# The prompt's own attention moved between the value tiles of the projection; eight equal steps a head in the attention stage

## The reference, cut to what matters

```python
# x_prompt: 128 tokens, x_sample: 1024 latent tokens, D = 1024, 8 heads; layer 1 is differential attention
qp, kp, vp, gp = attn_project(hp, w_in_attn)             # prompt: no rotary positions
op = diff_head_out(diff_attend(qp, kp, vp, lam), gp, subln, lam_init, w_out_attn)
qs, ks, vs, gs = attn_project(hs, w_in_attn)
qs, ks = apply_rope(qs), apply_rope(ks)
k_all, v_all = concat(ks, k_ctx), concat(vs, v_ctx)      # 1024 latent + 128 cached keys
os = diff_head_out(diff_attend(qs, k_all, v_all, lam), gs, subln, lam_init, w_out_attn)
# diff_attend: s = q k / sqrt(128) for both halves c of a head; p = softmax(s)
#              a = p[0] - lam * p[1];  o = a v
# diff_head_out: rms_norm(o) * subln * (1 - lam_init), then (o * silu(g)) @ w_out
```

## Time and profile before

| | us |
|---|---|
| median of 3 runs | 2426.21 (2423.43 to 2427.76) |
| the profiled execution | 2420.99 |
| its span | 2419.2 |
| TensorE busy | 2236.9 |
| VectorE busy | 1133.1 |
| ScalarE busy | 779.5 |

### The profile page before, as it was taken

How to read it: one execution, slowest core, us unless ns; L and a number is a source line. 1 busy time by engine, 2 the same in 40 slices (tenths; PEclk the granted TensorE clock), 3 DMA queues, 4 the chain that set the end, 5 groups by cost and what they waited for, 6 DMA issues and landing times. The chain is left out here.

```text
span 2419.2 us, 33660 instructions
## 1 busy us (share of the span) xinstructions
PE 2236.9 (92%) x13793; PEld 2138.6 (88%) x13793; DVE 1133.1 (47%) x1559; ACT 779.5 (32%) x1323; POOL 162.4 (7%) x68
## 2 busy tenths in 40 slices
PE   6799969988996999999999999989999999998996
PEld 1799947987996999999999999988888888888995
DVE  2835196374112644454411122237777777774112
ACT  2421043214112321111222121125666666664111
POOL 0200000000102121211200000000000000000100
PEclk9899889898998999999999999999999999999997
DMA  6554154177222445555542264361444443305224
GB/s 275 206 168 162 60 200 162 60 256 275 80 96 96 148 117 157 173 146 147 132 128 101 83 236 145 118 222 56 163 166 166 166 146 124 144 5 210 102 74 176
DMA packets 124603, 353.62 MB, mean 146 GB/s; under 512 B 12624, under 2 KB 62928, under 8 KB 116304
## 3 DMA queue, kind: packets, MB, share of 16 engines
q1 hardware_dynamic: 123344, 347.41, 41.8%
q10 hardware_dynamic: 1152, 4.72, 0.5%
HBM read 237.23 MB, written 114.82 MB: 146 GB/s over the span
## 5 line engine op out<-in xcount | busy, mean ns | idle before, releaser
L516 PE MATMUL p_ps<-p_h_hi,p_w_hi 128*128 128x384 f32 x1536 | 351.7, 336 | 33.3 <-DVE p_h_lo L616 33.3
L516 PE MATMUL p_ps<-p_h_lo,p_w_hi 128*128 128x384 f32 x1536 | 350.5, 336 | 0.0
L516 PE MATMUL p_ps<-p_h_hi,p_w_lo 128*128 128x384 f32 x1536 | 350.1, 335 | 0.0
L516 PEld LDWEIGHTS p_ps<-p_h_hi,p_w_hi 128*128 128x128 f32 x1536 | 275.4, 189 | 36.6 <-issue 28.5
L516 PEld LDWEIGHTS p_ps<-p_h_lo,p_w_hi 128*128 128x128 f32 x1536 | 275.5, 189 | 0.0
L516 PEld LDWEIGHTS p_ps<-p_h_hi,p_w_lo 128*128 128x128 f32 x1536 | 275.2, 189 | 0.0
L1371 PE MATMUL o_ps<-o_y_hi,o_w_hi 128*128 128x384 f32 x768 | 176.9, 338 | 25.3 <-DVE o_w_lo L1425 23.6
L1677 PE MATMUL a_ps<-a_v_hi,a_at_hi 128*128 128x256 f32 x584 | 178.8, 306 | 10.6 <-DVE a_g L1847 9.3
L1726 ACT ACTIVATE a_e<-a_ps,a_nmax 128x1152 f32<-128x1152 f32 (+1 forms) x143 | 161.3, 1128 | 69.6 <-DVE a_nmax L1792 69.6
L1792 DVE TENSOR_REDUCE a_nmax<-a_ps 128x1 f32<-128x1152 f32 (+1 forms) x143 | 176.3, 1233 | 4.0 <-PE a_ps L1640 1.6
L1371 PE MATMUL o_ps<-o_y_lo,o_w_hi 128*128 128x384 f32 x768 | 175.8, 336 | 0.0
(11 more groups left out here) (223 smaller groups left out, 3877.9 us busy)
## 6 DMA issues: line engine op xcount, KB each, us to landing
p_w_raw<-w_in_dram SPq DMA_DIRECT2D x40, 1024.0 KB, 6.1
g_dram<-p_stage SPq DMA_DIRECT2D x32, 576.0 KB, 3.0
f_w_raw<-w_u_dram SPq DMA_DIRECT2D x32, 512.0 KB, 3.6
o_w_raw<-w_out_dram SPq DMA_DIRECT2D x32, 512.0 KB, 4.3
f_g<-g_dram SPq DMA_DIRECT2D x8, 1152.0 KB, 7.7
y_dram<-f_y SPq DMA_DIRECT2D x8, 1152.0 KB, 5.3
x_dram<-o_x_new SPq DMA_DIRECT2D x16, 576.0 KB, 5.1
q_hi_dram<-p_cut_hi SPq DMA_DIRECT2D x32, 288.0 KB, 4.4
```

The source lines that it names most:

```text
L516: mm = pe.matmul(ps[:, 4 * b + c, 0:CH], a, x[:, c * CH:(c + 1) * CH], start=(d == 0 and j == 0), stop=(d == DT - 1 and j == 2))
```

## The change

The ninth step is taken out of the attention stage and done in the value unit of its head, and the rest follows from it:

- In a value unit the prompt's tile comes first (`ORDER`), then the eight latent ones. After the tile at place `at` TensorE, ScalarE and VectorE each do a piece of the prompt's attention of this head (`own_attention`): scores after place 0, maximum at 1, exponentials at 2, combination at 3, transpose and its two parts at 5, value product and norm at 6, scaling at 7, transposes of the output and gate at 8. Scores are now 128 columns wide. Two more PSUM banks (3 and 7) are used, and small tiles over parts of `stage` and of the past keys' split.
- SP loads the prompt's columns of q, k and g for head n + 1 at the start of unit n (`load_own`: four DMAs of 128 KB in 512-byte rows, one of 128 KB), and for head 0 in `after`, behind the first head's tiles. It first waits for the stores of all units ahead of the values. It stores the prompt's y of a head (`store_own`) one unit later.
- The value tiles are stored in the layout (head, partition, tile, column), in seven DMAs a unit (five and two) instead of six.
- In the attention stage every step has three groups and 1152 keys, 16 steps for two heads. `HeadTiles.load` takes 1024 queries, 1024 and 128 keys, twelve DMAs for a head; values have nine tiles, g and y the latent tokens only.
- 21 semaphores more are cleared between the two stages.

```diff
 class HeadTiles:
...
-            for what, size, into in (("q", T, self.q), ("k", KALL, self.k)):
+            for what, size, into in (("q", NS, self.q), ("k", KEYS, self.k)):
...
-            eng.dma_start(q, self.q_d[part][n, half]).then_inc(arrived, 16)
+            eng.dma_start(q, self.q_d[part][n, half][:, 0:NS]).then_inc(arrived, 16)
...
-            eng.dma_start(k[:, KEYS:KALL], self.k_d[part][n, half][:, NS:T]).then_inc(arrived, 16)
...
 def project(...):
...
+            SCORE, TURN = 3, 7
+            ORDER = [TT - 1] + list(range(TT - 1))
...
                 sp.wait_ge(past_out, 16 * 4)
+                for b in range(2):
+                    sp.wait_ge(stored[b], plan[3]["stored"][b])
                 ahead(sp)
+                load_own(0)
+
+            def load_own(n):
+                s = n % 2
+                for tiles, src in zip(own_qk, (heads.q_d, heads.k_d)):
+                    for tile, part in zip(tiles, src):
+                        sp.dma_start(tile[:, s].bitcast(F32), part[n].rearrange("c p t -> p c t")[:, :, NS:T]).then_inc(own_in[s], 16)
+                sp.dma_start(own_g[:, s], heads.g_d[n][:, :, NS:T]).then_inc(own_in[s], 16)
...
+                        if n >= 1:
+                            store_own(n - 1)
+                        if n + 1 < H:
+                            load_own(n + 1)
...
-                        for t in range(TT):
-
-                            pe.wait_ge(drained[p], k["drain"][p] + i * TT + max(t - 2, 0))
+                        for at, t in enumerate(ORDER):
+                            pe.wait_ge(drained[p], k["drain"][p] + i * TT + max(at - 2, 0))
...
                             mm.then_inc(proj_done, 1)
+                            own_attention(n, at, k["drain"][p] + i * TT)
...
+            def own_attention(n, at, drained_ahead):
+                s = n % 2
+                if at == 0:
+                    pe.wait_ge(own_in[s], 80 * (n // 2) + 80)
+                    pe.wait_ge(own_gated, n)
+                    for half in range(2):
+                        for j, (a, x) in enumerate(passes(*(part[:, s, half, :] for part in own_qk[0]),
+                                                          *(part[:, s, half, :] for part in own_qk[1]))):
+                            mm = pe.matmul(ps[:, SCORE, half * P:(half + 1) * P], a, x, start=(j == 0), stop=(j == 2),
+                                           skip_group_check=True)
+                    mm.then_inc(own_scored, 1)
+                if at == 5:
+                    pe.wait_ge(own_combined, n + 1)
+                    pe.wait_ge(own_scaled, n)
+                    pe.transpose(ps[:, TURN, 0:P], own_e[:, 0, :], sh.ident[:, :]).then_inc(own_turned, 1)
+                if at == 6:
+                    pe.wait_ge(own_lo, n + 1)
...
+                        mm = pe.matmul(ps[:, TURN, P:P + UC], a, x, start=(j == 0), stop=(j == 2), skip_group_check=True)
+                    mm.then_inc(own_multiplied, 1)
+                if at == 8:
+                    pe.wait_ge(own_scaled, n + 1)
+                    for h in range(2):
+                        mm = pe.transpose(ps[:, SCORE, UC + h * P:UC + (h + 1) * P], own_o[:, h * P:(h + 1) * P], sh.ident[:, :])
+                    mm.then_inc(own_back, 1)
...
 def attention(...):
...
-        def groups(m):
-            return [(KT - 1,)] if m % TT == TT - 1 else [(0, 1, 2, 3), (4, 5, 6, 7), (8,)]
...
+        STEPS = 2 * QT
+        GROUPS = [(0, 1, 2, 3), (4, 5, 6, 7), (8,)]
...
-                chunks = [(c, c * CH, CH) for c in range(NCH)] if t < TT - 1 else [(0, NS, UC)]
```

More of the change, by code:

```diff
@@ L278, in _, with project @@
             dve.scalar_tensor_tensor(sc, sc, 1.0, sh.norm_g[:, 0], ALU.add, ALU.mult).then_inc(dve_step, 1)
-def project(nc, sh, layer, x_src, w_src, kinds, rope, out, w_ada=None, past=None, ahead=None):
+def project(nc, sh, layer, x_src, w_src, kinds, rope, out, w_ada=None, past=None, ahead=None, heads=None):
     with ExitStack() as ctx:
@@ L314, in project @@
         v_new = sb("v_new", [P, UC]) if rope is not None else None
+        if rope is not None:
+            own_at_hi, own_at_lo = (sb(n, [P, P], F32R) for n in ("own_at_hi", "own_at_lo"))
+            own_nmax, own_lsum, own_linv = (sb(n, [P, 2]) for n in ("own_nmax", "own_lsum", "own_linv"))
+            own_ratio, own_osum, own_olog, own_orstd, own_ofac = (
+                sb(n, [P, 1]) for n in ("own_ratio", "own_osum", "own_olog", "own_orstd", "own_ofac"))
+            own_qk = [[nc.alloc_sbuf_tensor_at(f"p1_own_{what}{part}", [P, 2, 2, P], F32R,
+                                               offset=sh.base + 38912 + 2048 * (2 * w + p))
+                       for p, part in enumerate(("hi", "lo"))] for w, what in enumerate("qk")]
+            spare = stage[:].rearrange("p a t -> p (a t)")
+            own_g, own_y = (spare[:, 512 * n:512 * n + 512].rearrange("p (s a b) -> p s a b", s=2, a=2) for n in range(2))
+            own_e = spare[:, 1024:1280].rearrange("p (a b) -> p a b", a=2)
+            own_o, own_junk = spare[:, 1280:1536], spare[:, 1536:1792]
         wada = sb("wada", [P, 2, 2 * D]) if w_ada is not None else None
@@ L350, in project @@
         past_out = sem("past_out")
+        if rope is not None:
+            own_in = [sem(f"own_in{s}") for s in range(2)]
+            own_scored, own_maxed, own_expd, own_inverted, own_weighed, own_combined, own_turned = (
+                sem(f"own_{n}") for n in ("scored", "maxed", "expd", "inverted", "weighed", "combined", "turned"))
+            own_hi, own_lo, own_multiplied, own_squared, own_logged, own_rooted, own_factor, own_scaled, own_back, own_gated = (
+                sem(f"own_{n}") for n in ("hi", "lo", "multiplied", "squared", "logged", "rooted", "factor", "scaled",
+                                          "back", "gated"))
+            own_out = [nc.alloc_semaphore(f"p1_own_out{s}") for s in range(2)]
+            SCORE, TURN = 3, 7
+            ORDER = [TT - 1] + list(range(TT - 1))
         scaled = sem("scaled")
@@ L361, in project @@
         for n, (what, name, units) in enumerate(kinds):
-            stores = {"plain": 1, "silu": 1, "rope": 6 if name == "k" else 4, "value": 3}[what]
+            stores = {"plain": 1, "silu": 1, "rope": 6 if name == "k" else 4, "value": None}[what]
             per = TT if what == "value" else 2
@@ L371, in project @@
                 drain0[s] += units if what != "value" else units // 2 * TT
-                stored0[s] += 16 * stores * units
+                stored0[s] += 16 * units * (stores if what != "value" else V_STORES[s])
         def loops(eng, body, after=None):
@@ L1676, in apply @@
                                                           v_hi[:, s, kt, :], v_lo[:, s, kt, :])):
-                            mm = pe.matmul(ps[:, OB, 0:UC], a, x, start=(kt == groups(m)[0][0] and j == 0),
-                                           stop=(kt == total and j == 2))
-                    if n == len(groups(m)) - 1:
+                            mm = pe.matmul(ps[:, OB, 0:UC], a, x, start=(kt == 0 and j == 0),
+                                           stop=(kt == TT - 1 and j == 2))
@@ L1880 @@
     **{f"{what}_{part}": (H, 2, 2, P // 2, T) for what in "qk" for part in ("hi", "lo")},
-    **{f"v_{part}": (H, T, UC) for part in ("hi", "lo")},
+    **{f"v_{part}": (H, P, TT, UC) for part in ("hi", "lo")},
     **{f"{what}_past_{part}": (P, H * UC) for what in "kv" for part in ("hi", "lo")},
@@ L1939, in build @@
                  **{n: a[n] for what in "kv" for n in (f"{what}_past_hi", f"{what}_past_lo")}},
[L1940 removed]
+                past={"k": a["cache_k"], "v": a["cache_v"]}, ahead=first_head, heads=keys_in)
         sh.close_stage(nc)
         first_y = OutTiles(nc, sh, 1)
[L1943 removed]
+        attention(nc, sh, keys_in, by_part("v", "n p t v -> n p t v"), by_part("v_past", "p (n v) -> n p v", n=H),
                   tiles(a["g1"]), tiles(a["y1"]), lambda eng: first_y.load(eng, a["y1"], a["w_out1"]))
```

210 lines of the change are left out of this document (123 added, 87 removed).

## The result

| | before | changed |
|---|---|---|
| median of the runs | 2424.82 us (2422.87 to 2427.76, 4 runs) | 2409.15 us (2406.77 to 2410.38, 4 runs) |
| the profiled execution, time / span | 2420.99 / 2419.2 | 2410.38 / 2408.6 |

The ratio is 0.9933, with a 95% interval from 0.9916 to 0.995: 15.7 us or 0.65% faster, beyond the 0.2% that a measurement can tell. The forecast was 10.1 us or 0.42%, at 2416.1, and its range (2404 to 2424) holds the time. (The median before was 2426.21 over the three runs that the forecast started from; the fourth makes it 2424.82.)

A forecast was written before the change was run, and what follows sets the result against it. TensorE, busy 92% of the span, was taken as the bound; -49.7 - 3.1 + 16.1 + 23.3 + 2.5 + 0.8 = -10.1 us gave 2410.9 against the profiled 2420.99, carried by 5.2 to 2416.1 us, range 2404 to 2424.

The forecast's parts named there:

- Term 1: Attention stage, first to last gate: eight equal steps a head take 496.3 us instead of 546.0, a gain of 49.7 us.
- rival (d): Attention stage: half of the 6.15 us belongs to the change of heads and stays; 2440.7 us, chance 0.03.
- the prediction's other figure, 47.3: Attention stage: the gain in us if the clock falls all the same at the first gate, losing 2.4 us.
- Term 2: First gate of the attention stage: 1152 KB less in the queue ahead of and with g, a gain of 3.1 us.
- Term 3: Value units: the prompt's work between value tiles costs TensorE 2.01 us a head, 16.1 us for eight.
- the low end: Value units: 128-column score matmuls step at 0.111 us, so the prompt's work costs 1.39 us a head, 11.1 in all.
- ScalarE's cover: End of each value unit: the scaled output is ready 0.8 us before TensorE asks for it, so the chain costs nothing.
- Term 4: First value unit: TensorE waits 23.3 us for prompt tiles queued behind large loads, plus 2.5 us restarting at half clock.
- Rival (c): First value unit: it hardly waits because the small tiles overtake the large ones; 2390.3 us, chance 0.04.
- Term 5: Stage boundary: POOL clears 21 more semaphores at 0.036 us a piece, a cost of 0.8 us.

The follow-up runs named there:

- e4: Changed kernel with the past values' stores and head 0's prompt query and key loads moved ahead of the g units: 2381.45 us (ratio 0.982).
- e3: Changed kernel without the prompt's own attention in the value units (loads and engine work cut, stores kept): 2373.54 us (ratio 0.9792).
- e2: Changed kernel with each of the six 128-column score matmuls of a head's prompt issued twice: 2414.36 us (ratio 0.9961).
- e7: Changed kernel with one table set for logarithm and exponential loaded once at the start of the value units: 2410.95 us (ratio 0.9932).
- e5: Changed kernel with an extra logarithm and exponential, each with its table load, in every unit's ScalarE chain: 2431.98 us (ratio 1.0027).
- e8: Changed kernel with head 0's g loaded ahead of head 1's queries and keys in the attention stage: 2404.84 us (ratio 0.9913).
- e9: Changed kernel run again without any edit: 2406.82 us (ratio 0.9933).
- e1: Changed kernel with head 0's five small prompt loads issued ahead of the first head's twelve large loads: 2396.99 us (ratio 0.9892).
- e6: e4 with head 0's g loaded ahead of head 1's queries and keys in the attention stage: 2381.87 us (ratio 0.9811).
- e11: e6 run again without any further edit: 2380.30 us (ratio 0.9816).

## Why the prediction was right, and where it was off

The sign, the mechanism and the place of every large term hold. The gain was put 5.6 us too low (10.1 of 15.7), and that is the balance of several errors. By the table, against the first profile:

- **Term 1** (49.7): 48.7 from gate to gate. That the prompt's step cost 6.15 us a head, and eight equal steps 7.90 each, is right, and rival (d) falls. What failed is "I take it that the clock then stays at 2.4 GHz": the first interval is 9.43, because a wait of 2.0 us on TensorE is left. Over the profiles, waits of 1.1 and 1.4 us there left it at 7.9, waits of 2.0 to 2.6 gave 9.4, and 3.6 to 3.7 gave 10.3 to 10.6. The changed kernel's second profile has such a wait (3.58), and its gates take 47.2 us less than before: there the prediction's other figure, 47.3, holds. The last intervals are 0.8 us shorter together than taken.
- **Term 2** (3.1): 4.2 measured. What counts is when the first gate can run, and that was and is when g lands: 27.24 us after SP's first load of the stage before, 23.08 after in both profiles of the changed kernel, and 23.2 to 23.6 in the seven others with this order of loads. So the queue gave 3.6 to 4.2 us. The wait in brackets fell by 3.15, close to the forecast, but that is luck: it also holds how early the chain ahead of the gate was done, and in the second profile of the same kernel it is 3.81 with the gate no later. The sum took 1.18 MB less at 386 GB/s. In the windows up to the gate the rate holds, and the bytes moved before g is there fell by 1.5 MB; where the 0.3 MB more than counted lie stays open.
- **Term 3** (16.1): 10.6 measured, e4 against e3. This is the step that was furthest off: "narrow matmuls run in another way than wide ones, so I take 0.215". They step at 0.11 (e2), the bound that was kept as the low end; with it the term is 11.1. The 66 columns of the earlier trace rows had already cost no more than the 2 columns, and a pace that doesn't change between 2 and 66 columns was better evidence than a difference of durations, since matmuls overlap. 0.215 is what they take at half clock, and it was met there by chance. The rest, the transposes and the three 256-column matmuls, was put at 0.72 and measured 0.65 (1.33 less 0.68). ScalarE's cover was 1.2 us, where 0.8 was worked out; the cost of nothing holds (e7), and e5 shows what lies beyond it. The drain of 1380 ns for each switch, which the Trainium skill gives ("ScalarE: Activation LUTs", "What ACT_TABLE_LOAD costs"), does not show: in a unit of e5 four loads of 1.28 us and four activations, in turn, take 6.2 us in all (1478.18 to 1484.38), and no gap in them is over 0.03 us.
- **Term 4** (23.3 + 2.5): 24.57 and 3.0. The five other profiles with this wait had 23.3 to 24.3 (e2, e5, e7, e8, e9), so the size lies within 1.3 us; and what the value stage of e2, e7, e8 and e9 lost beyond wait and matmuls, against e4, is 2.0 to 3.0. e1 and e4 show that the cause is the one given, the order and the place of the issues in the one queue, behind the past values' stores and the first head's loads. Rival (c) falls.
- **Term 5** (0.8): nothing. The boundary's 0.40 us between SP's issues is the same with 21 semaphores more. A difference between two boundaries had been divided by their semaphores, though they differ in more.
- **Not in the sum:** the value stage without any of the prompt's work is 1.5 us shorter than before (e3). Of these, 0.7 lie between the first and the last value matmul (207.92 us before, 207.23 in e3), where the second unit no longer holds a wait. The other 0.8 lie between the last value matmul and SP's first load (4.01 and 3.20), where the copy of the new values has gone (0.3), and SP's last three issues take 1.58 us instead of 2.11 (0.5).

So -10.1 becomes -10.1 + 1.0 - 1.1 - 5.5 + 1.8 - 0.8 - 1.5 = -16.2 us. That the two profiled executions differ by 10.6 us, close to the forecast, is luck: 5.6 us went to stretches without a change.

## What to carry to other kernels

Work moved into a stage that TensorE fills is paid in full, and here it was worth it, 10.6 us for 48.7; the larger loss, 27.6 us, came from where the moved work's first loads stood in the queue. Ask of every moved step when its first inputs are issued and what stands ahead of them: tiles that can be filled a stage earlier cost nothing there. And count a wait of TensorE with its restart: 1.8 us of waiting cost 1.7 more in clock here, and 23 to 25 cost 2 to 3.

## What the runs showed of the hardware that was not expected

- A wait of 1.8 us, repeated in each unit, cost 3.5 us a unit through the granted clock (e5), while waits of 1.1 and 1.4 us at the first gate cost only themselves (e1, e5).
- The same code with the same waits does not always meet the fall of the clock: it came behind seven of eight equal waits in e5, and in the last steps of the attention stage in e6, e7, e8 and e11, in e9 by 0.25 us, and not in the other seven. It is worth 1.1 to 1.7 us where it comes in full. Together with the spread of the untouched columns it leaves effects under 3 us unproved by medians of five.
- Matmuls of 128 float32r columns step at 0.11 us at full clock, as those of 2 and 66 do, and the 256-column ones at 0.12.
